# Four of eight row-block pairs of the gate/up products by seven products, and four of eight plain half groups with accumulated low parts

## The reference

```python
def swiglu_ffn(x, norm_g, w_gate, w_up, w_down):
    h = rms_norm(x, norm_g)
    return (jax.nn.silu(h @ w_gate) * (h @ w_up)) @ w_down

def reference(x, ...):
    for layer in range(DEPTH):          # 2
        ...                             # layer 0: chunked_sgu_mixer, layer 1: moba_attention
        x = x + swiglu_ffn(x, ffn_norm[layer], ffn_w_gate[layer], ffn_w_up[layer], ffn_w_down[layer])
    return x
```

## Time and profile before

| | |
|---|---|
| median of 3 runs | 2087.15 us |
| profiled execution | 2086.11 us |
| its span, first to last instruction | 2084.4 us |
| TensorE busy | 2078.1 us |
| VectorE busy | 1607.0 us |
| ScalarE busy | 1154.7 us |
| GpSimd busy | 77.2 us |
| DMA, mean moved | 203 GB/s |
| granted TensorE clock | 1.00 |

### The profile page before, as it was taken

The page is one execution under the profiler, slowest core; times in us unless marked ns, Lnnn a source line. Parts: engine busy times, 40 slices in busy tenths (PEclk is TensorE's granted clock), DMA queues, the critical chain, the costliest instruction groups (busy, mean ns, idle before and its releaser), DMA issues.

```text
span 2084.4 us, 24295 instructions
## 1 busy us (share of the span) xinstructions
PE 2078.1 (100%) x9454; PEld 1724.9 (83%) x9454; DVE 1607.0 (77%) x1777; ACT 1154.7 (55%) x1402; POOL 77.2 (4%) x87
## 2 busy tenths in 40 slices
PE   9999999999999999999999999999999999999999
PEld 8888888888888888888888888888888888888887
DVE  5466578889888897888566666578889888887887
ACT  6444556555556554646666655466555556554653
POOL 2000000000000000000011001000000000000000
PEclk9999999999999999999999999999999999999999
DMA  9655547666676667655554454447666676667654
GB/s 329 206 174 180 180 146 254 227 202 207 217 240 204 210 213 225 211 191 202 194 185 166 150 191 164 163 162 250 220 204 213 209 235 204 220 210 229 207 193 150
DMA packets 209373, 424.16 MB, mean 203 GB/s; under 512 B 8720, under 2 KB 9328, under 8 KB 209008
## 3 DMA queue, kind: packets, MB, share of 16 engines
q1 hardware_dynamic: 202720, 398.50, 55.4%
q0 software_dynamic: 6544, 24.16, 5.5%
HBM read 399.56 MB, written 2.10 MB: 193 GB/s over the span
## 4 chain that ended last, share of the span: by engine, by line
PE 98%; DVE 1%; ACT 0%; DMA 0%; SPq 0%; issue 0%
PE acc L1586 19%; PE acc L1588 19%; PE acc L1587 19%; PE acc L1445 10%; PE acc L1449 10%; PE acc L1447 10%; PE tr L1588 2%; PE tr L1586 2%; PE tr L1587 2%; PE tr L1493 2%; PE tr L1753 0%; DMA raw<-in_a_w_in_dram 0%; PE tr L1556 0%; PE tr L1727 0%; PE tr L1737 0%; PE tr L1745 0%
## 5 line engine op out<-in xcount | busy, mean ns | idle before, releaser
L729 ACT ACTIVATE w_hi<-raw 128x1024 fp32r<-128x1024 f32 x360 | 367.0, 1052 | 198.5 <-PE acc L1588 185.1
L1136 DVE TENSOR_TENSOR w_lo<-raw,w_hi 128x1024 fp32r<-128x1024 f32 x320 | 379.8, 1220 | 30.1 <-ACT w_hi L729 30.1
L1586 PE MATMUL acc<-w_hi,a_hi 128*128 128x512 f32 x896 | 350.4, 391 | 0.0
L1588 PE MATMUL acc<-w_hi,a_lo 128*128 128x512 f32 x896 | 348.8, 389 | 0.0
L1587 PE MATMUL acc<-w_lo,a_hi 128*128 128x512 f32 x896 | 348.6, 389 | 0.0
L1445 PE MATMUL acc<-w_hi,a_hi 128*128 128x512 f32 x640 | 254.6, 398 | 0.2 <-DVE a_lo L968 0.2
L1449 PE MATMUL acc<-w_hi,a_lo 128*128 128x512 f32 x640 | 249.7, 390 | 0.0
L1447 PE MATMUL acc<-w_lo,a_hi 128*128 128x512 f32 x640 | 249.2, 389 | 0.0
L942 DVE TENSOR_TENSOR w_lo<-raw,w_hi 128x1024 fp32r<-128x1024 f32 x127 | 153.5, 1225 | 118.0 <-ACT w_hi L567 118.0
L718 ACT ACTIVATE s_hi<-raw 128x1536 fp32r<-128x1536 f32 x84 | 124.7, 1484 | 187.5 <-PE acc L1588 187.5
L718 ACT ACTIVATE s_hi<-sums_b 128x1024 fp32r<-128x1024 f32 x168 | 172.7, 1055 | 72.0 <-DVE sums_b L1131 64.6
(11 more groups left out here) (219 smaller groups left out, 3513.7 us busy)
## 6 DMA issues: line engine op xcount, KB each, us to landing
raw<-in_ffn_w_down_dram SPq DMA_DIRECT2D x68, 1024.0 KB, 5.0
raw<-in_ffn_w_gate_dram SPq DMA_DIRECT2D x46, 1024.0 KB, 5.2
raw<-in_ffn_w_up_dram SPq DMA_DIRECT2D x46, 1024.0 KB, 5.1
raw<-in_ffn_w_gate_dram SPq DMA_DIRECT2D x84, 512.0 KB, 4.4
raw<-in_ffn_w_up_dram SPq DMA_DIRECT2D x84, 512.0 KB, 5.5
raw<-in_a_w_in_dram SPq DMA_DIRECT2D x30, 1024.0 KB, 5.3
w_lo<-raw POOLq DMA_DIRECT2D x40, 512.0 KB, 4.4
raw<-in_ffn_w_down_dram SPq DMA_DIRECT2D x40, 512.0 KB, 4.8
```

The source lines that it names most:

```text
L729: nc.scalar.activation(w_hi[:, m % RING, :, :], src, ACT.Copy).then_inc(hi_split, 1)
L1136: nc.vector.tensor_tensor(w_lo[:, m % RING, :, :], raw[:, slot, half * HG:(half + 1) * HG, :], w_hi[:, m % RING, :, :].bitcast(F32), ALU.s ...
L1586: nc.tensor.matmul(bank[:, :], hi, rhs_hi, start=start, stop=False)
L1588: return nc.tensor.matmul(bank[:, :], lo, rhs_hi, start=False, stop=stop)
```

## The change

In the blocks of kind "chunk" (c = 1 to 10, both layers, 20 blocks) four pairs go by seven products where three did, and eight plain half groups are left of ten. Of these, g4, g5, g7 and u7 get their low part from an accumulating transfer, where g5 and g6 did. ScalarE has an order of its own in these blocks (u7 ahead of u6). There is one plain half group between two pairs, where there were two. A slot of `raw` is now free only when every item of its load is done. Since a fourth set of forms must fit, the fourth form of each pair is kept in the place of a left operand block that no plain product reads, so the casts and subtractions of the forms are cut into two or three instructions.

```diff
-    WINO, WINO_H = 3, 2
+    WINO, WINO_H = 4, 2
...
-              "chunk": items("g3 g4 g5 g6 s0 g7 u7 s1 u3 u4 s2 u5 u6"),
+              "chunk": items("g4 g5 g6 s0 g7 s1 u4 s2 u5 s3 u6 u7"),
...
-             "chunk": loads_of("g3 g4,g5 g6,s0,g7 u7,s1,u3 u4,s2,u5 u6"),
+             "chunk": loads_of("g4 g5,g6 g7,s0,s1,u4 u5,s2,s3,u6 u7"),
...
-    ADDED = {"chunk": items("g5 g6"), "first": [], "down 0": [], "down 1": [], "down middle": []}
+    ADDED = {"chunk": items("g4 g5 g7 u7"), "first": [], "down 0": [], "down 1": [], "down middle": []}
+    ACT_ORDERS = {"chunk": items("g4 g5 g6 g7 s0 s1 u4 s2 u5 s3 u7 u6")}
...
             def forms_hi_part(n, dst, fourth, rest=None):
                 act.wait_ge(forms_ready, n)
-                nc.scalar.activation(dst[:, :, :], sums_b[:, 0:dst.shape[1], :], ACT.Copy).then_inc(forms_hi, 1)
+                pairs_n = dst.shape[1]
+                nc.scalar.activation(dst[:, :, :], sums_b[:, 0:pairs_n, 0:3 * P], ACT.Copy)
+                ins = nc.scalar.activation(fourth, sums_b[:, 0:2, 3 * P:4 * P], ACT.Copy)
+                if rest is not None:
+                    ins = nc.scalar.activation(rest[:, :, :], sums_b[:, 2:pairs_n, 3 * P:4 * P], ACT.Copy)
+                ins.then_inc(forms_hi, 1)
...
-                            hooks = {("g", 4): [lambda: read_p1((layer, "chunk", c - 1))], ("g", 5): [lambda: silu(c - 1)],
+                            hooks = {("g", 5): [lambda: read_p1((layer, "chunk", c - 1))], ("g", 6): [lambda: silu(c - 1)],
                                      ("s", 0): [lambda: hidden_hi(c - 1, c0)]}
...
-                            hooks = {("g", 6): [lambda: sums(k, 0)], ("u", 7): [lambda: sums(k, 1)],
-                                     ("u", 4): [lambda: sums(k, 2)]}
+                            hooks = {("g", 7): [lambda: sums(k, 1)], ("u", 4): [lambda: sums(k, 2)],
+                                     ("u", 5): [lambda: sums(k, 3)]}
                             if c > c0:
-                                hooks[("g", 4)] = [lambda: gate_sums(c - 1)]
-                                hooks[("g", 5)] = [lambda: hidden(c - 1)]
-                                hooks[("g", 6)].insert(0, lambda: dve.wait_ge(staged, b0 + c - NC))
+                                hooks[("g", 5)] = [lambda: gate_sums(c - 1)]
+                                hooks[("g", 6)] = [lambda: hidden(c - 1), lambda: dve.wait_ge(staged, b0 + c - NC),
+                                                   lambda: sums(k, 0)]
```

More of the change, by code:

```diff
@@ L128, in yoco_kernel @@
         reads = SLOT_READ[layer]
-        reads += [("half group", hg - 6 + 2 * n) for n in range(RAW)]
+        reads += [[("half group", hg - 6 + 2 * n)] for n in range(RAW)]
         for p, (c0, c1) in enumerate(PARTS):
@@ L140, in yoco_kernel @@
                     DOWN_LOAD.setdefault((layer, p), []).append(len(reads) - RAW)
-                    reads += [("half group", hg + 2 * g + 2) for g in range(c1 - c0)]
+                    reads += [[("half group", hg + 2 * g + 2)] for g in range(c1 - c0)]
                     hg += 2 * (c1 - c0)
@@ L162, in yoco_kernel @@
                         LOAD_OF[k, item], BOTH_OF[k, item] = len(reads) - RAW, n_both[slot]
[L163 to L166, removed]
+                    reads.append([("pair", PAIR_OF[k, item[1]] + 1) if item[0] == "s" else
+                                  ("added", HG_OF[k, item]) if item in ADDED[kind(k)] else
+                                  ("half group", HG_OF[k, item] + 1) for item in load])
         assert hg % RING == 0 and len(reads) % RAW == 0
@@ L303, in yoco_kernel, with in_place, h_spare @@
         x_banks = [None, acc[2], acc[1], tr]
+        def in_place(rows, first=0):
+            return rows[:, first:first + 4:2, P:2 * P]
+        def h_spare(p):
+            return 0 if p in DOWN_PAIRS else 4 * (PARTS[p][1] - PARTS[p][0])
         def x0_bank(kk):
@@ L390, in slot_free @@
             def slot_free(layer, n):
[L392 to L398, removed]
+                for what, count in SLOT_READ[layer][n - RAW]:
+                    if what == "pair":
+                        sp.wait_ge(s_split, count)
+                    elif what == "added":
+                        sp.wait_ge(lo_added[count % RING], 16 * n_added(count))
+                    else:
+                        sp.wait_ge(lo_split, n_split(count))
             def block_loads(k, w_first, w_second, n):
@@ L757, in block_hi @@
                 def block_hi(k, hooks):
-                    for item in order(k):
+                    for item in ACT_ORDERS.get(kind(k), order(k)):
                         slot, count = in_slot(LOAD_OF[k, item])
@@ L790, in feed_forward @@
                                   ("u", 2): [lambda: hidden_hi(c1 - 1, c0)],
[L791 removed]
+                                  ("u", 3): [lambda: forms_hi_part(FORMS[layer, "down", p, 0], fh_hi, in_place(h_hi))]})
                         block_hi((layer, "down", p, 1), {("g", 3): [lambda: read_p1((layer, "down", p, 0))]})
@@ L1644, in block_products @@
                         if m == "s":
-                            pair(PAIR_OF[k, q], operands, q, q == 0, q == pairs(k)[-1], "u" not in begun,
+                            pair(PAIR_OF[k, q], operands, q, q == 0, q == pairs(k)[-1], not begun & {"u", "first of u"},
                                  tr_read if q == 0 else None)
@@ L1700, in feed_forward @@
                          {0: b0 + c1 - 1, n - 2: b0 + c1}, j0=first, n=n)
-                    block_products(km, (h_hi, h_lo, fh_hi, fh_lo), b_end + 1 if layer == 0 else b0 + c1, {
+                    block_products(km, (h_hi, h_lo, h_form), b_end + 1 if layer == 0 else b0 + c1, {
                         ("u", 2): [lambda: pe.wait_ge(staged, b0 + c1 - NC)],
```

72 lines of the change are left out of this document (45 added, 27 removed).

## The result

The changed kernel takes 2150.8 us (median of 4 runs, 2145.8 to 2158.0) against 2087.0 for the kernel before (2086.7 to 2087.2): ratio 1.031, 95% interval 1.028 to 1.033. It is slower by 64 us, where 2086.1 was predicted. The profiled execution took 2158.0, with a span of 2156.3; it is the longest of the four. They differ with the granted clock: 2145.8 and 2146.8 us go with a mean of 0.994 and 0.995, 2154.8 and 2158.0 with 0.990 and 0.988.

A forecast was written before the change was run, and what follows sets the result against it. TensorE, busy 2078.1 of 2084.4 us, was taken as the bound. Span 2084.4 - 13.6 + 10.8 + 1.8 + 0 = 2083.4; adding 1.7 and 1.04 gave 2086.1 us, range 2079 to 2097.

The forecast's parts named there:

- Products removed, -13.6: TensorE, 20 chunk blocks: 183 products become 180, block 42.40 to 41.72 us, -13.6 us in all.
- Forms at 0: Forms cut in pieces, one more pair's forms made: under 1 us on waiting engines, taken as 0; other end +8.
- The chain of 42.6, +10.8: VectorE-ScalarE handoffs through a changed block sum to 42.6 us, over TensorE's 41.72; waits 5.4 per layer, 10.8 in all.
- the foretold waits of 0.1 to 0.2 on s_lo: Sign: TensorE waits 0.1 to 0.2 us each in front of the pairs' first products, 10 us in all.
- if they are on w_lo from transfers instead, the third term is the larger: Sign: TensorE's waits on w_lo would mean the accumulating transfers, put at +1.8, are the larger term.
- The accumulating transfers, +1.8 (0 to +10): DMA: transfers go from 40 to 80; lateness beside weight loads taken as 0.3 us a run over six runs.
- one load in front: Upper bound for the transfers: the whole 1.05 MB load goes first, 2.7 us, making g5 1.7 us late.
- That is paid once per run and not per block: Transfer lateness counted for six runs only, since the VectorE-ScalarE chain was said not to wait for TensorE.
- The rule on turns by whole packets: DMA engines alternate rings by packets of about 9 to 17 descriptors; an accumulate waits for at most one other packet.
- Rival 2: Load for s0 delays u7's transfer or slows all three; g5 1.7 late, +10.2, 2094.5; chance 0.22, plus 0.04 beyond 2120.

The follow-up runs named there:

- where loads are short: Changed kernel, but in chunk blocks after the first each weight load moves half its bytes: 2117.5 us, ratio 1.0145.
- the one with the held load: Kernel with transfers of g7 and u7, load of s0 issued only once the previous block's u7 transfer landed, within a run: 2108.3 us, ratio 1.0105.

## Why the prediction was wrong

- **Products removed, -13.6: right in the block, 3.6 short in the span.** With g6 and g7 as transfers, the changed kernel's products run without a wait, in blocks of 41.7 us (transposes at 630.21 and 671.94), as forecast. The span is 2074.4, so 10.0 came.
- **Forms at 0: mis-sized in one of the two layers.** Between that kernel and the one before, the transposes behind the first block of the first layer come 0.47 us later (337.10 against 336.63), but so do all transposes ahead of it, from 140.60 against 140.13 on: the forms cost nothing there, and the 0.47 comes from the program's start. In the second layer the offset goes from -5.07 (1349.37 against 1354.44) to -4.46 over the first two blocks, of which the second saves 0.68: about +1.3. TensorE waits 1.34 us there for a w_lo of VectorE (1393.65), which stands close behind the pieces of the forms. Most of the rest lies in seven blocks that save less than 0.68 each, 1.8 us together; why they do was not traced, but for one wait of 0.4 on a transfer.
- **The chain of 42.6, +10.8: its length right, its weight never felt.** 42.55 was measured where loads are short. In the changed kernel a longer loop of 46.0 covers it, and the foretold waits of 0.1 to 0.2 on s_lo don't appear; of the signs listed, "if they are on w_lo from transfers instead, the third term is the larger" is what came.
- **The accumulating transfers, +1.8 (0 to +10): the step that failed.** Three parts of it were wrong. First the order at the DMA engines. The earlier trace rows do show two queues taking turns: q1 had loads pending there (those issued at 42.03 and 46.76 landed after 11.8 and 9.6 us). But both queues had long begun. What the step needed was how long a transfer waits for its first packet, and the same trace has that 9 us ahead of the earlier trace rows: GpSimd's transfer of 36.89 us, behind a load of 1 MB issued at 35.91, got no packet up to 40 us (queues from 37 to 40):

```profile
q1 hardware_dynamic: 414, 0.85, 96.6%
```

In the changed kernel u7's transfer got nothing for 4.5 us in the same way. Second the size: one load in front was the right number, but its 2.7 us were packet time at full rate. The first packet of the transfer came 5.0 us after its issue in place of 1.4, so 3.6 later, and the load beside it was slower too (its halves landed after 4.2 and 5.8 us, and after 3.6 and 4.5 where it was held back). u7's landing went from 4.4 to 9.0, and g5 was not the first to be late. Third, "That is paid once per run and not per block". The argument looked at the VectorE-ScalarE chain alone. The loop through u7's products is 4.4 + 2.72 + 32.55 = 39.7 us with a quick transfer and passes 42.6 once the landing is above 7.3; so it was open by 2.9 us, and the transfer grew by 4.6. The 1.7 beyond that and the 1.7 of slower products are the way from 42.6 to 46.0.

- **The clock was no term at all.** The waits are 54.7 us, but the changed kernel is 81.9 above the one with g6 and g7 (2156.3 against 2074.4), 1.5 us for each us of wait; the kernel with g7 and u7 75.7 for 54.6; the one with the held load 31.3 for 19.9. The mean granted clock of 0.988, 0.992 and 0.994 in the three makes some 26, 17 and 13 us of these.
- **The rule on turns by whole packets** (the Trainium skill, "DMA: Bandwidth & Descriptors", section "Queues, rings and completion order") agrees with the stretches in which both queues have begun (131 and 137 packets, 79 and 80). It did not give the wait before a transfer's first packet: the trace shows 482 pieces of some 2 KB of the other queue first, 30 for each of the 16 engines. If such a piece is what the page calls a descriptor, that is two to three of its typical packets, where the prediction reckoned with one at most.
- **Rival 2** had the place (the load of s0 ahead of u7's transfer) and its condition, a landing above 5.1, but priced it at g5 and once per run, and gave only 0.04 to a time above 2120.

Neither queue goes first as a rule. In the kernel before, the load issued at 42.03, behind transfers of GpSimd's queue, had to wait in its turn (41 to 45 us):

```profile
q0 software_dynamic: 305, 1.46, 99.5%
q1 hardware_dynamic: 1, 0.00, 0.0%
```

Left open: what sets the order of two transfers issued within some tenths of a microsecond. u7's transfer waited for the second half of the load of s0 too, which was issued 0.14 us behind it; the load issued 0.38 behind it, in the kernel with u7 ahead of s3, did not go first as a whole. Why a load beside a waiting transfer is itself slower is open as well.

## What to carry to other kernels

Before moving work to an accumulating transfer, list the loads issued within some microseconds ahead of and beside each transfer, and price it at its own time plus theirs, with the time to landing and not that of the packets alone; then ask how far away its reader is. Here the same 20 transfers cost 75 us when they were read 6.4 us after their issue and nothing at 11.8, by one swap in one engine's order. A wait that is fed back, from a late product through the sums to the next transfer, is paid in each round, and in these kernels each us that TensorE waited cost 1.4 to 1.6. Equal packet counts of two queues that have both begun say nothing of how long a newcomer waits for its first packet: look at the stretch behind its issue.

## What the runs showed of the hardware

- An accumulating transfer of 512 KB lands 4.4 us after its issue when no load is queued, and 8.4 to 10.1 with 1 MB issued beside it (the kernel with g7 and u7). Its first packet comes 1.4 us after its issue when alone, at most 2.7 with 0.5 MB beside it, and 4.8 to 5.1 with 1 MB.
- The reverse holds too: a load of 1 MB issued while two accumulating transfers are under way needed 8.4 to 8.7 us, and one issued behind three transfers of GpSimd's queue 11.8.
- Once both queues have begun they are served in turns: 79 and 80 packets in 2 us, 131 and 137 in 3 us.
- After 2.4 us of idle TensorE the granted clock was 0.50 in the window of 645 to 647 us, 0.89 in the next and 1.00 from 649; after another wait of 2.4 us it stayed at 1.00 (690.25). In the changed kernel it fell at 12 of the 20 waits, which were 2.0 to 4.1 us long. In the kernel without accumulating transfers 18 waits of at most 0.7 us (10.0 us in all) left the mean clock at 1.000.
